# Strips behind the gate products split in the last pair, attention's last unit at other parts of a pooling strip, a weighted sum in whole operations

## What is computed

```
u = rmsnorm(h);  q, k, v, pz, ga, gp = split(u @ w_in)
for g, (window, dilation) in enumerate(((128,1), (512,4), (2048,16))):
    outs[g], lses[g] = dilated_window_attention(q_g, k_g, v_g)     # 4 heads of 64 each
a = sum_g softmax_g(lses)[g] * outs[g]                              # 256 channels
p = (trailing_mean(pz, windows 2, 4, 8, 16) - pz) @ w_grp * scale   # 768 channels
merged = sigmoid(ga) * (a @ w_att_out) + sigmoid(gp) * (p @ w_pool_out)
h = h + merged @ w_out
```

## Time and profile before

| | |
|---|---|
| median of 3 runs | 3312.97 us (3310.12 to 3313.02) |
| the profiled execution | 3312.09 us, span 3310.3 us |
| TensorE | busy 3254.9 us (98%) |
| VectorE | busy 1852.1 us (56%) |
| ScalarE | busy 1344.6 us (41%) |
| GpSimd | busy 1340.7 us (41%) |
| mean granted clock of TensorE | 0.995 |

### The profile page before, as it was taken

How to read it: one execution, slowest core, us unless ns; L and a number is a source line. 1 busy time by engine, 2 the same in 40 slices (tenths; PEclk the granted TensorE clock), 3 DMA queues, 4 the chain that set the end, 5 groups by cost and what they waited for, 6 DMA issues and landing times.

```text
span 3310.3 us, 48566 instructions
## 1 busy us (share of the span) xinstructions
PE 3254.9 (98%) x19078; PEld 2630.8 (79%) x19078; DVE 1852.1 (56%) x2490; ACT 1344.6 (41%) x2134; POOL 1340.7 (41%) x835
## 2 busy tenths in 40 slices
PE   9999999999999999999999999999999999999998
PEld 6877787777778888888788878878876888888886
DVE  6333325655457778777692446304473266555678
ACT  5333324343325464333443455214423353444544
POOL 4322115545322846454425655521112665444102
PEclk9999999999999999999999999999999999999999
DMA  4221213232437332333553334311342432445664
GB/s 128 75 65 59 71 52 113 79 106 74 137 105 263 96 95 80 99 96 120 205 177 99 101 116 129 106 53 60 102 127 93 134 96 71 133 147 197 222 193 149
DMA packets 405538, 382.54 MB, mean 116 GB/s; under 512 B 19104, under 2 KB 323104, under 8 KB 402496
## 3 DMA queue, kind: packets, MB, share of 16 engines
q1 hardware_dynamic: 385248, 338.54, 33.2%
q10 hardware_dynamic: 20064, 40.90, 3.5%
HBM read 292.44 MB, written 86.93 MB: 115 GB/s over the span
## 4 chain that ended last, share of the span: by engine, by line
PE 44%; DVE 5%; issue 1%; ACT 1%; DMA 1%; POOL 0%; DVEq 0%; ACTq 0%
PE psum L2149 19%; PE psum L5133 10%; PE psum L2789 7%; PE psum L3402 3%; PE psum L1736 2%; PE psum L1779 1%; PE psum L2825 1%; DVE gate L4573 1%; PE psum L1766 0%; DVE conv L3164 0%; PE psum L1754 0%; DVE acc L5169 0%; PE psum L1756 0%; DVE w_lo L2683 0%; ACT w_hi L2081 0%
## 5 line engine op out<-in xcount | busy, mean ns | idle before, releaser
L2100 POOL TENSOR_TENSOR w_lo<-w_raw,w_hi 128x1024 fp32r<-128x1024 f32 (+1 forms) x232 | 563.6, 2430 | 1031.3 <-ACT w_hi L2081 1029.3
L2081 ACT ACTIVATE w_hi<-w_raw 128x1024 fp32r<-128x1024 f32 (+1 forms) x233 | 240.9, 1034 | 449.9 <-PE psum L2149 397.6
L291 PE MATMUL psum<-x_hi,w_hi 128*128 128x512 f32 x832 | 354.0, 425 | 3.7 <-ACT gate L335 3.5
L2149 PE MATMUL psum<-x_hi,w_hi 128*128 128x512 f32 x912 | 343.6, 397 | 8.6 <-POOL w_lo L2100 4.9
L2149 PE MATMUL psum<-x_lo,w_hi 128*128 128x512 f32 x912 | 338.3, 391 | 0.0
L2149 PE MATMUL psum<-x_hi,w_lo 128*128 128x512 f32 x912 | 337.9, 390 | 0.0
L291 PE MATMUL psum<-x_hi,w_lo 128*128 128x512 f32 x832 | 326.1, 392 | 0.0
L291 PE MATMUL psum<-x_lo,w_hi 128*128 128x512 f32 x832 | 325.6, 391 | 0.0
L2149 PEld LDWEIGHTS psum<-x_hi,w_hi 128*128 128x128 f32 x912 | 171.1, 188 | 49.1 <-issue 11.1
L2149 PEld LDWEIGHTS psum<-x_lo,w_hi 128*128 128x128 f32 x912 | 172.2, 189 | 37.6 <-issue 2.2
L2149 PEld LDWEIGHTS psum<-x_hi,w_lo 128*128 128x128 f32 x912 | 171.9, 188 | 36.2
(11 more groups left out here) (844 smaller groups left out, 7820.1 us busy)
## 6 DMA issues: line engine op xcount, KB each, us to landing
w_raw<-in_w_in SPq DMA_DIRECT2D x105, 512.0 KB, 4.5
merge_raw<-gates ACTq DMA_DIRECT2D x48, 512.0 KB, 3.7
x_raw<-mlp_forms SPq DMA_DIRECT2D x76, 256.0 KB, 3.5
gates<-gate SPq DMA_DIRECT2D x32, 512.0 KB, 2.9
w_raw<-in_w_mlp_out SPq DMA_DIRECT2D x54, 256.0 KB, 3.1
mlp_forms<-mlp_staged SPq DMA_DIRECT2D x13, 1024.0 KB, 4.0
w_raw<-in_w_ffn_up SPq DMA_DIRECT2D x24, 512.0 KB, 3.8
ffn_x_raw<-ffn_forms SPq DMA_DIRECT2D x46, 256.0 KB, 3.9
```

The source lines that it names most:

```text
L291: last = pe.matmul(bank, w[:, k, :], x[:, k, half(h)], start=(k == 0 and j == 0), stop=(k == KT - 1 and j == 2))
L2081: act.activation(self.view(self.c.wh, i), self.view(self.c.wr, i), ACT.Copy).then_inc(self.sig["w_hi"], 1)
L2100: pool.tensor_tensor(self.view(self.c.wl, i), self.view(self.c.wr, i), self.view(self.c.wh, i).bitcast(F32), ALU.subtract).then_inc(self.s ...
L2149: last = pe.matmul(self.bank(t, h)[0:m, :], w[:, k, col:col + m], x(k)[:, 512 * h:512 * h + 512], start=(k == 0 and n == 0), stop=(k == nk ...
```

## The change

It has three parts. The two strips behind the gate products are split by ScalarE inside the last pair's row, the first behind product 4, the second behind product 6, and no longer behind the store of "c12". GpSimd's list is not touched; its two splits follow the signals. `tensor_end` puts the last unit's turn and the weighing of the unit before it ahead of part 1 of the first pooling strip (it was part 4), and the last unit's weighing ahead of part 3 (it was part 7). And `AttentionMerge.vector` multiplies a group by its weights in one operation over all blocks, with the same elements in the same order.

```diff
--- before.py
+++ after.py
@@ -1796,10 +1796,10 @@
 
     def tensor_end(self, pe, k):
 
-        if k == 4:
+        if k == 1:
             self.turn(pe, self.N - 1)
             self.weighted(pe, self.N - 2)
-        if k == KT - 1:
+        if k == 3:
             self.weighted(pe, self.N - 1)
 
     def left(self, pe, s):
@@ -3418,7 +3418,7 @@
         row = (self.first + 2 * p + n) * P
         act.dma_start(self.gates[row:row + P, half(h)], src).then_inc(self.sig[f"gate_{name}_stored"], 16)
 
-    def scalar(self, act, p):
+    def scalar(self, act, p, after=None):
         self.store(act, p - 1, "c12")
         for n, u in enumerate(self.blocks[p]):
             self.done(act, p, n)
@@ -3432,6 +3432,8 @@
                 self.store(act, p, "c22")
             if n == 6:
                 self.store(act, p, "c21")
+            if after:
+                after(n)
 
     def vector(self, dve, p):
         after = self.blocks[p + 1] if p + 1 < self.count else None
@@ -4286,12 +4288,13 @@
                     feed2.hi(act, 0)
             for u in range(1, feed2.PLACES):
                 feed2.hi(act, u)
+            def resume(act, n):
+                if n in (4, 6):
+                    at = st.holds[1][0] + (n - 4) // 2
+                    st.hi(act, st.ends[at - 2], at + 1, True)
             for p in range(sevens.count):
-                sevens.scalar(act, p)
+                sevens.scalar(act, p, (lambda n: resume(act, n)) if p == sevens.count - 1 else None)
             sevens.store(act, sevens.count - 1, "c12")
-            for i in range(2):
-                at = st.holds[1][0] + i
-                st.hi(act, st.ends[at - 2], at + 1, True)
             sevens.all_stored(act)
             for n in range(6):
                 qkv.take_v(act, n)
@@ -4497,12 +4500,19 @@
         for g in range(3):
             link(dve.tensor_tensor(w[:, g], w[:, g], r[:, 2], ALU.mult))
         for g in range(3):
-            for j in range(NC):
-                dst = (acc if g == 0 else tmp)[:, j, :].rearrange("p (h e) -> p h e", e=64)
-                link(dve.tensor_tensor(dst, grp[g][:, j, :, 0:64], bcl(w[:, g, j, :], 64), ALU.mult))
+            link(dve.tensor_tensor(self.heads(acc if g == 0 else tmp), self.values(g), self.share(g), ALU.mult))
             if g:
                 link(dve.tensor_tensor(acc[:, :, :], acc[:, :, :], tmp[:, :, :], ALU.add))
         dve.sem_inc(sig["merged"], 1)
+
+    def heads(self, buf):
+        return buf[:, :, :].rearrange("p j (h e) -> p (j h) e", e=64)
+
+    def values(self, g):
+        return self.groups[g][:, :, :].rearrange("p j (h e) -> p (j h) e", e=66)[:, :, 0:64]
+
+    def share(self, g):
+        return bcl(self.w[:, g].rearrange("p j h -> p (j h)"), 64)
 
     def weigh(self, act):
         act.wait_ge(self.sig["diff"], 1)
```

## The result

The changed kernel takes 3292.93 us (median of 4 runs, 3291.99 to 3295.63), the kernel before in the same comparison 3311.55 (3308.37 to 3313.02). The ratio is 0.9946, with a 95% interval of 0.9929 to 0.9964. The profiled execution took 3295.63 us, with a span of 3293.8; for a profiled execution the forecast was 3296.2.

The account below looks back on a forecast made before the run. TensorE, busy 98% of the span, was taken to bound the kernel through its waits and the slow clock behind them. Gains of 6.7 + 9.2 = 15.9 us gave 3297.1 us, range 3295 to 3299.5 (chance 0.78), widened to 3294.5 to 3301.

Parts of the forecast that it names:

- The first gap: TensorE's wait for `w_lo` between the last gate product and the first v tile, with slow clock behind: 6.7 us gained.
- The last unit: Attention's last weighing moved earlier in the first pooling strip: 5.58 us sooner less a new 0.6 us wait, so 5.0 us.
- the second rival: TensorE's wait for `a_lo` stays, as the third group's store and reload take the time given back: 3306.3 us, chance 0.03.
- The whole operations: VectorE's weighted sums before `a_lo`: 2.29 us per operation instead of 3.65 for eight small ones, three times, saving 4.1 us.
- The rival with a much slower form: Whole operation with repeated weights runs at a much lower rate; at 10 us each 3317.7 us; slower has chance 0.02.
- one of the long additions may be held by a split: VectorE's additions of 2048 elements: one took 4.37 us against 2.29 while GpSimd split a strip; shared ports exclude each other.
- The margin of `a_lo`: Before the merge, `a_lo` is ready ahead of TensorE's need, with 2.5 us to spare, so wait and slow clock go.
- `a_lo` may move by some 2.1 us either way: VectorE's windows and weighted sums meet other GpSimd splits than before, shifting `a_lo` by some 2.1 us.
- The merge: From TensorE's pooling strips through sigmoid and gatings to `tensor_mix`, at 2483.3 instead of 2492.47: 9.2 us gained.
- The half microsecond added for loads that have less time: Allowance of half a microsecond ahead of `tensor_mix`, moving its start from 2482.8 to 2483.3.
- the first rival: VectorE bounds the merge: `tensor_mix` starts at 2487.4, gain there only 5.1 us, time 3301.2 us; chance 0.12.
- against the median the forecast is 3297.1 us: Whole kernel: profiled 3312.09 us would become 3296.2; the shown runs' median of 3312.97, 0.9 above, gives 3297.1 us.

## Why the prediction was right, and where it was wrong

**The first gap.** Right. Forecast 6.7 us, measured 6.76, and 6.76 alone and 6.73 by its absence. The row of the profile that gave the slow clock its price (ten products in 3.96 us) was enough.

**The last unit.** Right: an idle time of 0.45 us at the turn, 0.65 with what it costs beside, where 0.6 was forecast, and the last weighing 4.80 us sooner where 5.0 was. The store and reload did not eat it, which was the second rival.

**The whole operations.** Right: 2.29 us each, 3 x 1.36 = 4.1 us. The rival with a much slower form is out. The forecast saw that one of the long additions may be held by a split, and the 4.36 us of L4505 are such a hold. The Trainium skill (SBUF — State Buffer, section "SBUF: two separate sides") describes the two engines' shared ports as an exclusive lock for a whole instruction, and the trace agrees on both sides: the split that started while a 2.29 us operation ran shows 3.24 us and not 2.39. It did no harm, as each split had its strip's 11 us.

**The margin of `a_lo`.** Forecast 2.5 us, measured 4.4. From the first pooling strip to `a_lo` are 64.71 us where they were 75.75, 11.04 less, and the forecast had 5.0 + 4.1 = 9.1. 4.80 are the weighing and 4.1 the operations; the other 2.1 are one split of GpSimd that no longer falls on this chain. In the kernel before the three small operations on the weights are held by one:

```profile
2416.01 2.75 DVE L4498 TENSOR_TENSOR beside_weights<-beside_weights,beside_sums 128x32 f32<-128x32 f32 x3
```

In the changed kernel they take 0.65. Before, five rows between the weights and `a_lo` were longer than their like by about 2 us; now it is four, and it is four too in both kernels that undo half of the second part. The prediction said that `a_lo` may move by some 2.1 us either way through this; it moved by just that, and nothing of it shows in the time, since the first gating waits for the sigmoid and not for VectorE.

**The merge.** Nearly right. First gating 4.4 us behind the strips (forecast 4.3), from there to the end of the fifth 15.9 (16.0), then 2.87 to `tensor_mix` (2.9). The half microsecond added for loads that have less time was not needed: a load does end ScalarE's wait, but no later than before. That half, forecast at 0.5 and measured at nothing, is nearly the whole difference between 9.2 and 9.71, and the one term of the sum of the gain that was clearly mis-sized. "VectorE becomes the bound of the merge", the first rival, did not come about in the changed kernel at its price of 4.1 us, though VectorE still ends a wait of 0.93 us there; what comes nearer to it are the two kernels in which the last unit's move or the whole operations are missing, at 2.6 and 3.1 us.

**The step that failed** is the last: "against the median the forecast is 3297.1 us", and with it the lower end of the range. The steps of the gain hold. It is 16.5 us in the trace, 0.6 over the forecast, and the profiled execution took 3295.63 us where the forecast for it was 3296.2 (it was the slowest of the four runs). In the first comparison the medians differ by 18.6 us, 2.1 more than the trace gives. The rest of the miss is in the base and the spread. The median of three runs, 3312.97, stood 2.5 us above the 3310.47 that 35 runs give. Subtracting the forecast 15.9 from this gives 3294.6; with the measured 16.5 it gives 3294.0, and the 14 runs of the changed kernel have 3293.4. Four runs of one kernel spread over 3.6 us here, so of the 4.2 us of the miss 2.5 are the base, 0.6 the gain, 0.6 what marks and medians differ by, and 0.5 that the four runs first shown stood below the fourteen. The range gave 2.6 us below, 1.4 of them for a merge without waits, which left 1.2 for the spread. The three runs shown already spread over 2.9 us, and all 35 over 7.0. With so wide a spread it is partly chance on which side of 3294.5 a median of four falls: two of the changed kernel's three medians (3292.93, 3295.02, 3293.20) lie below it.

## What to carry to other kernels

Price a wait by the stretch between two marks around it that every kernel passes: such a stretch repeats to 0.01 us here, while whole times of one kernel spread over 4 to 7, and a base taken from three runs brings its own error into the forecast. A long wait costs itself and the slow clock behind it (4.91 us cost 6.7). Two savings on one chain don't add: the first takes the wait away, the second only what idle time and held operations behind it leave.

## What the runs showed of the hardware that was not expected

A wait of 2.53 us was followed by products at 1.2 GHz (windows at 0.82 and 0.76), while waits of 1.46, 1.50 and 1.69 us left the clock at 1.00. But the length of a wait doesn't settle it: one and the same wait of 1.87 us at 38 us was followed by a window at 0.86 in six profiles and at 1.00 in the other six. After equal waits of 7.46 and 7.45 us the stretch to `tensor_mix` differed by 0.86 us.

Very short operations on VectorE are held as well as long ones: beside a split on GpSimd a copy of two elements lasted 2.24 us and an operation of 16 elements 2.07, where they take 0.17.
